# Folding the block-diagonal weights of a recurrent mixer into its gate and score weights, taking square roots on the raw sums, and a later start for a scaling on GpSimd

## The reference, cut to what matters

```python
def block_diag_linear(x, w):                      # w: 512 blocks of 4 x 4
    xb = x.reshape(x.shape[:-1] + (nb, bi))
    return jnp.einsum('...ni,nio->...no', xb, w).reshape(x.shape[:-1] + (nb * bo,))

def mlstm_block(h, w_up, conv_w, conv_b, wq, wk, wv, w_gates, b_gates, ...):
    xm, z = jnp.split(h @ w_up, 2, axis=-1)       # 256 x 2048 each
    xc = jax.nn.silu(causal_conv(xm, conv_w, conv_b))
    q = block_diag_linear(xc, wq)
    k = block_diag_linear(xc, wk)
    v = block_diag_linear(xm, wv)
    gates = q @ w_gates[:2048] + k @ w_gates[2048:4096] + v @ w_gates[4096:] + b_gates
    i_pre, f_pre = gates[:, :4], gates[:, 4:]     # log_sigmoid(f_pre): a softplus
    hh = mlstm_chunkwise(heads(q), heads(k), heads(v), i_pre, f_pre)   # 4 heads of 512
    hh = head_layer_norm(hh, norm_g) + skip * xc
    return (hh * jax.nn.silu(z)) @ w_down

def layer_norm(x, g, b):   # (x - mean) * rsqrt(var + 1e-5) * g + b
def rms_norm_2(x, g):      # x * rsqrt(mean(x * x) + 1e-6) * g
```

## Time and profile before

| | us |
|---|---|
| median of 3 runs | 2662.36 |
| the profiled execution, its own time | 2666.65 |
| its span (first to last instruction) | 2664.8 |
| PE busy | 2370.0 (89% of the span) |
| DVE busy | 1746.7 (66%) |
| ACT busy | 1198.4 (45%) |
| POOL busy | 221.5 (8%) |
| granted PE clock, mean | 0.937 of full speed |

### The profile page before, as it was taken

One profiled execution on the slowest core, in us unless ns is written; L12 is line 12 of the kernel. 1 busy time (PEld: TensorE's weight loads), 2 busy tenths in 40 slices (PEclk: granted clock), 3 DMA queues, 4 the chain that ended last, 5 costly groups with the idle time before them and its releaser, 6 DMA issues.

```text
span 2664.8 us, 34633 instructions
## 1 busy us (share of the span) xinstructions
PE 2370.0 (89%) x14138; PEld 2071.4 (78%) x14138; DVE 1746.7 (66%) x2134; ACT 1198.4 (45%) x1410; POOL 221.5 (8%) x234
## 2 busy tenths in 40 slices
PE   5779889996878899997899887899989989998997
PEld 5667778885656778886899786789979989367997
DVE  2557557887477566887776766677667765156554
ACT  2353335674344335675433564243343345343432
POOL 4001001211001001220000012000000020300000
PEclk9788999997798899999999998999999999988999
DMA  7315667894303766897686432368668734003651
GB/s 182 127 69 186 216 221 285 316 329 177 112 1 136 256 236 242 313 329 259 221 278 228 144 111 95 126 227 280 221 215 288 253 124 165 32 1 127 199 189 64
DMA packets 241166, 504.89 MB, mean 189 GB/s; under 512 B 10287, under 2 KB 104497, under 8 KB 241008
## 3 DMA queue, kind: packets, MB, share of 16 engines
q1 hardware_dynamic: 216128, 417.84, 45.3%
q10 hardware_dynamic: 21456, 77.09, 8.2%
q0 software_dynamic: 3424, 7.75, 1.3%
HBM read 501.59 MB, written 1.05 MB: 189 GB/s over the span
## 4 chain that ended last, share of the span: by engine, by line
PE 42%; DVE 7%; ACT 3%; issue 1%; ACTq 0%; DVEq 0%
PE PS L990 19%; PE PS L1005 9%; PE PS L831 5%; PE PS L791 3%; DVE WGL L2131 1%; PE PS L1415 1%; DVE AR L2134 1%; PE PS L1510 1%; PE PS L1027 1%; DVE X L2131 1%; DVE XN L2131 1%; ACT WGH L1598 1%; PE PS L1460 1%; DVE XTL L2131 1%; PE PS L1438 0%
## 5 line engine op out<-in xcount | busy, mean ns | idle before, releaser
L2131 DVE TENSOR_TENSOR WGL<-ring,WGH 128x2048 fp32r<-128x2048 f32 x258 | 589.4, 2289 | 308.0 <-ACT WGH L1598 173.1
L990 PE MATMUL PS<-XTH,WGH 128*128 128x256 f32 x1408 | 403.3, 286 | 7.7 <-DVE XTL L2131 7.6
L990 PE MATMUL PS<-XTL,WGH 128*128 128x256 f32 x1408 | 401.0, 285 | 0.0
L990 PE MATMUL PS<-XTH,WGL 128*128 128x256 f32 x1408 | 400.9, 285 | 0.0
L990 PEld LDWEIGHTS PS<-XTH,WGH 128*128 128x128 f32 x1408 | 272.9, 194 | 13.8 <-issue 9.7
L990 PEld LDWEIGHTS PS<-XTL,WGH 128*128 128x128 f32 x1408 | 272.8, 194 | 4.1 <-issue 1.0
L990 PEld LDWEIGHTS PS<-XTH,WGL 128*128 128x128 f32 x1408 | 272.7, 194 | 0.0
L2131 DVE TENSOR_TENSOR WDL<-ring,WDH 128x1024 fp32r<-128x1024 f32 (+1 forms) x136 | 217.1, 1597 | 63.2 <-ACT WDH L1751 46.3
L1751 ACT ACTIVATE WGH<-ring 128x2048 fp32r<-128x2048 f32 x96 | 183.4, 1912 | 165.6 <-PE PS L1055 99.0
L1598 ACT ACTIVATE WGH<-ring 128x2048 fp32r<-128x2048 f32 (+1 forms) x74 | 138.4, 1876 | 200.6 <-PE PS L813 73.9
L1790 ACT ACTIVATE XN<-PS 128x256 f32<-128x256 f32 x88 | 33.7, 383 | 358.0 <-PE PS L990 326.2
(11 more groups left out here) (494 smaller groups left out, 5357.3 us busy)
## 6 DMA issues: line engine op xcount, KB each, us to landing
FA<-in_ada_w ACTq DMA_DIRECT2D x144, 512.0 KB, 6.3
ring<-in_moe_w_up SPq DMA_DIRECT2D x64, 1024.0 KB, 7.0
ring<-in_moe_w_gate SPq DMA_DIRECT2D x64, 1024.0 KB, 7.3
ring<-in_moe_w_down SPq DMA_DIRECT2D x64, 1024.0 KB, 6.3
ring<-in_ffn_w_gate SPq DMA_DIRECT2D x44, 1024.0 KB, 5.6
ring<-in_ffn_w_up SPq DMA_DIRECT2D x44, 1024.0 KB, 9.4
ring<-in_ffn_w_down SPq DMA_DIRECT2D x44, 1024.0 KB, 7.3
ring<-in_hyb_w_in SPq DMA_DIRECT2D x10, 1152.0 KB, 6.6
```

What stands on the lines that cost most here:

```text
L990: ins = mm(PS[:, 4 + b, m * T:(m + 1) * T], w_[:, b, w], x_[:, k, :], start=k == 0 and q == 0, stop=k == KD - 1 and q == 2)
L2131: return V.tensor_tensor(out_, x_, y_, op)
```

## The change

**Folding.** At the start of the kernel, behind POOL's small loads, ten POOL instructions (L688 to L701 of the changed kernel) multiply the gate weights, loaded now in another layout in 12 loads of 128-byte pieces (`G4`), by the 4x4 blocks, and leave in `WGT` weights that apply to `XC` and `XM` directly; four more loads (`K4`) and the same instructions put the product of the q and k blocks into `WQKV[0]`. The 12 loads of `WGT` are gone. A new semaphore, `fold`, counts to 10; DVE waits for it ahead of the attention of `even` (the loads lie in `XN`), PE ahead of the first gate product. The gates are now 32 products instead of 48 + 48, and they stand within the projection: one behind each of tiles 4 to 19 (with `XM`), four behind each of tiles 13, 16, 20 and 23 (with `XC`). `scores(h)` makes 4 products with ACT copies instead of 8 and uses `XC` as the keys. POOL makes 32 block-diagonal matrices instead of 96. ACT's Silu of `XC` stands at tiles 11, 14, 18 and 21 instead of 21, 24, 27 and 30; the gates are copied out at tile 24 and the softplus Exp stands at tile 25. DVE interleaves its softplus with the low parts of the last five pieces.

**Roots.** `root_of_variance` and `root_of_squares` give epsilon as the Sqrt's bias and (for the squares) 1/D as the Square's scale, so DVE's step on `VAR` and its mark are gone; `root_of_squares` begins with a 1x1 Sqrt ahead of the Squares.

**The scaling by GpSimd** waits, besides the transposes, for `m_route` (DVE's reordering of the routing) ahead of `moe0` and `moe1`, and for `x_low` (all of X split) ahead of `odd`. In `moe`, ACT's `trn_out` stands ahead of two of its high parts.

The diff, cut to its core:

```diff
@@ gpsimd: start of the kernel
-            for g in range(6):
-                for m in range(2):
-                    ld(WGT[:, g, m, :, :], a["mlstm_w_gates_2"][0][8 * g * P:8 * (g + 1) * P, 4 * m:4 * m + 4]
-                       .rearrange("(k p) e -> p k e", p=P), "small_load")
+            for i in range(4):
+                for w in range(3):
+                    ld(G4[i::4, 16 * w:16 * w + 16, :, :].rearrange("n k c e -> n k (c e)"),
+                       a["mlstm_w_gates_2"][0][2048 * w:2048 * (w + 1), :].rearrange("(t n c) e -> n t (c e)", n=32, c=4),
+                       "small_load")
+                ld(K4[i::4, :, :, :].rearrange("n k i c -> n k (i c)"),
+                   a["mlstm_wk_2"][0].rearrange("(t n) i o -> n t (i o)", n=32), "small_load")
...
+            pool.wait_ge(S("small_load"), 16 * N_SMALL)
+            gmul(G4, G4, bc(by_row.unsqueeze(3), (P, 48, 4, 8)), ALU.mult).then_inc(S("fold"), 1)
+            gmul(K4, K4, bc(WQKV[:, 0, :, :].unsqueeze(2), (P, 16, 4, 4)), ALU.mult).then_inc(S("fold"), 1)
...
@@ gpsimd: scaling of the residual
                     pool.wait_ge(S("xt_ps"), 4 * (plan[n + 1].u + 1))
+                    if plan[n + 1].kind == "moe":
+                        pool.wait_ge(S("m_route"), 5 * plan[n + 1].me + 4)
+                    else:
+                        pool.wait_ge(S("x_low"), plan[n + 1].sb + KD // 2)
@@ tensor: mlstm
                 for f in range(32):
                     project_tile(r, f, 6)
...
+                    if f == 4:
+                        pe.wait_ge(S("row"), r.v2 + 1)
+                        pe.wait_ge(S("fold"), N_FOLD)
+                    if 4 <= f < 20:
+                        pe.wait_ge(S("tile_out"), EV_BASE["mlstm"] + f - 3)
+                        gates_add(16 + f - 4, XM[:, f - 4, 3:])
+                    if f in (13, 16, 20, 23):
+                        h = (13, 16, 20, 23).index(f)
+                        pe.wait_ge(S("xc"), h + 1)
+                        for k in range(4 * h, 4 * h + 4):
+                            gates_add(k, XC[:, k, :])
...
-                for h in range(4):
-                    pe.wait_ge(S("bd"), h + 1)
-                    pe.wait_ge(S("xc"), h + 1)
-                    for w in range(3):
-                        for j in range(4):
...
@@ scalar
-            def root(out_, in_):
-                count["sqrt"] += 1
-                act.wait_ge(S("var"), count["sqrt"])
-                f(out_, in_, ACT.Sqrt).then_inc(S("sd"), 1)
+            def root_of_variance(eps):
+                count["var"] += 1
+                act.wait_ge(S("var"), count["var"])
+                f(SD, MV[:, :, 1], ACT.Sqrt, bias=eps).then_inc(S("sd"), 1)
+            def root_of_squares():
+                f(ST[0:1, 94:95], EPSC[0:1, 1:2], ACT.Sqrt)
+                for t in range(TT):
...
+                    f(XN[:, t, :], X[:, t, :], ACT.Square, scale=D ** -0.5, accum_out=SSQ[:, t:t + 1])\
+                        .then_inc(S("ssq"), 1)
+                act.wait_ge(S("ssq"), count["xres"])
+                f(SD, SSQ, ACT.Sqrt, bias=EPSC[:, 1:2]).then_inc(S("sd"), 1)
@@ scalar: mlstm
+                    if f_ == 24:
+                        act.wait_ge(S("gadd"), 32)
+                        f(SPX[4], PS[32:36, 6, 0:T], ACT.Copy).then_inc(S("f_row"), 1)
+                    if f_ == 25:
+                        softplus_exp(SPX[1], SPX[0])
@@ vector: mlstm
-                for p in range(10, r.n_proj + 2):
+                for p in range(10, 13):
                     low(r, p)
...
+                softplus(SPX[5], x_, *SPX[0:4], beside)
+                low(r, 15)
...
                 mark().then_inc(S("gtok_in"), 1)
+                low(r, 16)
+                low(r, 17)
```

More of the change, by code:

```diff
@@ L470, in program @@
         BLK = [(0, P), (P, MW)]
+        roots = []
+        for r in plan:
+            if r.kind in ("ffn", "hyb", "mlstm"):
+                roots.append((r.name, "begin"))
+            if r.name == "odd":
+                roots.append((r.name, "q"))
+            if r.name == "hyb":
+                roots += [(r.name, 0), (r.name, 1)]
+            if r.name == "mlstm":
+                roots += [(r.name, h) for h in range(4)]
+            if r.kind in ("even", "odd", "moe"):
+                roots.append((r.name, "ln"))
+        roots.append(("final", "begin"))
+        ROOT_AT = {x: n + 1 for n, x in enumerate(roots)}
         work = [r for r in plan if r.kind != "mod"]
@@ L1576, in squares @@
             def squares(r):
-                for t in range(TT):
-                    act.wait_ge(S("xres"), TT * r.v2 + t + 1)
-                    f(XN[:, t, :], X[:, t, :], ACT.Square, accum_out=SSQ[:, t:t + 1]).then_inc(S("ssq"), 1)
-                root(SD, VAR)
+                root_of_squares()
                 act.wait_ge(S("rstd"), r.v2 + 1)
@@ L1708, in odd @@
                       PS[0:HD, b, 0:m * T].rearrange("p (m t) -> p m t", m=m), ACT.Copy).then_inc(S("qit"), 1)
-                root(SD4, VAR4)
+                f(SD4, SSQ4, ACT.Sqrt, bias=EPSC[:, 1:2]).then_inc(S("sd"), 1)
                 act.wait_ge(S("odd_ps"), 2)
@@ L2005, in hyb @@
                     if f_ == LRU_AT + 12:
-                        root(RG, RG)
+                        act.wait_ge(S("lru_one"), 1)
+                        f(RG, RG, ACT.Sqrt).then_inc(S("lru_root"), 1)
                     if k == 1:
@@ L2027, in hyb @@
                         high(r, r.n_proj + 4)
-                root(H2_RS[:, 0, :], H2_RS[:, 0, :])
+                act.wait_ge(S("sq_out"), 1)
+                f(H2_RS[:, 0, :], H2_RS[:, 0, :], ACT.Sqrt).then_inc(S("sd"), 1)
                 high(r, r.n_proj + 5)
-                root(H2_RS[:, 1, :], H2_RS[:, 1, :])
+                act.wait_ge(S("sq_out"), 2)
+                f(H2_RS[:, 1, :], H2_RS[:, 1, :], ACT.Sqrt).then_inc(S("sd"), 1)
                 for p in range(r.n_proj + 4, len(r.pieces)):
@@ L2101, in final @@
             def final():
-                for t in range(TT):
-                    act.wait_ge(S("xres"), TT * v2_end + t + 1)
-                    f(XN[:, t, :], X[:, t, :], ACT.Square, accum_out=SSQ[:, t:t + 1]).then_inc(S("ssq"), 1)
-                root(SD, VAR)
+                root_of_squares()
             act.dma_start(CON[:, :], a["const"][:, 0:NCONST]).then_inc(S("con_load"), 16)
@@ L2134, in stt, with inverse, softplus @@
                 return V.scalar_tensor_tensor(out=out_, in0=x_, scalar=s, in1=y_, op0=o1, op1=o2)
-            def root(rstd, sd):
-                count["var"] += 1
-                mark().then_inc(S("var"), 1)
-                dve.wait_ge(S("sd"), count["var"])
+            def inverse(rstd, sd, name, what):
+                dve.wait_ge(S("sd"), ROOT_AT[name, what])
                 c(V.reciprocal(rstd, sd))
-            def softplus(out_, x_, a_, e, d, w):
+            def softplus(out_, x_, a_, e, d, w, beside=None):
                 count["sp"] += 1
@@ L2790, in hyb @@
                         c(stt(RG, H2, 1.0, RG, ALU.add, ALU.mult))
[L2791 to L2792 removed]
+                        mark().then_inc(S("lru_one"), 1)
                         mark().then_inc(S("hyb_made"), 1)
@@ L2937, in mlstm @@
                         c(V.bn_stats(BN[:, t, 0, :], HN[:, t, :]))
-                        c(V.bn_aggr(MV[:, t, :], BN[:, t, 0, :]))
-                    c(ts(VAR, MV[:, :, 1], EPS, None, ALU.add))
-                    root(RSTD, SD)
+                        ins = V.bn_aggr(MV[:, t, :], BN[:, t, 0, :])
+                        if t == 0:
+                            c(ins)
+                    ins.then_inc(S("var"), 1)
+                    inverse(RSTD, SD, "mlstm", h)
                     for t in range(TT):
```

187 lines of the change are left out of this document (87 added, 100 removed).

## The result

The changed kernel takes 2600.26 us (median of 4 runs, 2597.93 to 2606.41) where the kernel before takes 2663.16 (4 runs, 2659.74 to 2664.22): a ratio of 0.9771, 95% interval 0.9756 to 0.9786, so 62.9 us or 2.3% faster. The forecast was 2596 with a range of 2580 to 2613. The profiled execution took 2606.41, the longest of the four; its span is 2604.6 us.

The account below looks back on a forecast made before the run. TensorE's feed-forward and projection products bound the kernel and stay; gains lie between them. Terms 46.3 + 1.5 + 9.5 + 2.8 + 5.3 + 1.7 - 1 = 66.1 us, off the median 2662.36, give 2596; range 2580 to 2613.

Parts of the forecast that it names:

- the likeliest case: Whole kernel: all terms hold and the median falls from 2662.36 to 2596 us; chance 0.46.
- Step 1: mlstm, projection to first pm: softplus hidden, gate products between tiles, stalls of 1.6 and 4.3 us; 46.3 us saved.
- Step 2: Heads of mlstm: PE work halves but the table load waits for the variance; 1.5 us saved, bounds -1 and 5.
- Rival B: Heads: table load not held by the variance, heads 1 to 3 give 1.5 us each; 2593 us, chance 0.15.
- Step 3: Start of odd: late GpSimd scaling no longer stretches DVE's splitting of X; 9.5 us saved, bounds 3 and 10.
- Rival A: Start of odd: GpSimd's port hold moves to low parts, gain 1.5 us instead of 9.5; 2604 us, chance 0.12.
- Step 4: Start of moe0 and moe1: earlier ACT copies and unstretched DVE casts save 1.4 us each, 2.8 in all.
- Step 5: Roots on sums, seven stages: dummy Sqrt hides the table load in four, 1.15 us each, 0.25 elsewhere; 5.3 us saved.
- Step 6: Roots on variances: 0.28 us saved in each of four, plus 0.6 for the hybrid mixer's two roots.
- Step 7: Start of the kernel: some 4 us of GpSimd folding falls on low parts of even's projection; 1 us lost.
- Rivals C and E: C: start loads delay even's first weights, 2601 to 2611, chance 0.1; E: late fold delays even's attention, 2670, chance 0.02.
- Rivals D and F: D: mlstm's projection stalls more, 2601 to 2606, chance 0.1; F: softplus Exp or Silu waits stop PE, 2620, chance 0.05.

Follow-up runs that it names:

- the standard: The changed kernel measured again, unedited, as reference for later runs: 2598.87 us, ratio 0.9764 to the kernel before; its profiled execution took 2592.25 us.
- the first execution: Profiled execution from the first measurement of the changed kernel, with no further edit: 2606.41 us.

## Why the prediction was right

The forecast of the likeliest case came out, 66 us foreseen and 62.9 measured, and the mechanisms were those foreseen, with errors of size in both directions. Step by step:

- **Step 1, mlstm to the first pm**: 46.3 foreseen; 44.2 measured in the standard (185.2 to 141.0 us) and 41.5 in the first execution (143.6). The mechanism held to the single stall: 1.6 and 4.3 foreseen, 1.54 and 4.05 in the trace, and half clock around the second. The forecast counts "the next 12 us" at half clock behind PE's wait in the trace of before; there the clock fell 3.6 us before that wait ended and came back 10 us behind its end. Mis-sized was the term "32 gate products at some 0.5 us", 16 us: they took 19.2. The price of 0.5 holds for the groups (0.51); the 14 lone ones cost 0.73 each, for each brings its own change from fp32r products and back. The rest, from tile 24 to the first pm, was forecast at 41.4 with the clock, and took 40.2 in the standard and 43 in the first execution, where two more stretches of 3.4 us at half clock fell into scores(0). That the clock falls there in one execution and not in the other was in no term.
- **Step 2, the heads**: 1.2 of the 1.5 foreseen lay between the first and the last pm; 1.6 measured. Rival B (the load isn't held) is refuted by the load's row behind the aggregate, and the run that frees it shows what it would have been: 2.75 us more, where the rival had some 3 (2593 for 2596). That the load was held could be read only from the order of instructions, not from the trace of before. The sign of being wrong, a period under 14, was put carelessly: the step itself had 13.1 for head 1, and that came.
- **Step 3, odd**: 9.5 foreseen, 7.7 measured from trace to trace, 6.75 by undoing it. From the transposes to the high part the forecast had 12.5 us, the trace has 14.67. Of the 2.1 between them, 1.3 are the first product, 6.24 us behind the transposes and not 4.93: in odd it waits for ACT's last copy (the 2.57 in its row), in mlstm it didn't. The rest goes with the clock, granted at 0.50 from 641 to 653; at the start of mlstm it was back at full speed 8 us behind the transposes. Why it rose sooner there, no run tells. Rival A (the loss is only moved) is refuted as to time: GpSimd's hold did move to the low parts, but these had idle time ahead of them, and undoing the wait cost 6.75 us up to the high part and 8.0 in the stage.
- **Step 4, the experts' stages**: 1.4 each foreseen; the first expert product comes 2.3 to 2.5 us earlier (14.6 to 12.3 and 12.1), the next high part 1.2 us in moe0 and 2.85 in moe1. So the size was put too low, 2.8 for some 4 in both. The cause was half wrong: the step counted on DVE's casts, "freed of GpSimd's instructions"; with ACT's new order these didn't matter. That late scaling costs nothing there held, though low parts became 4.5 us long.
- **Step 5, roots on sums**: 1.15 a stage foreseen for four, 1.13 measured ahead of mlstm and 1.12 in the three others. All of it is the dummy's; without it the new root is 0.16 slower than the old one. In the three stages without a load 0.23 for 0.25.
- **Step 6, roots on variances**: aggregate to reciprocal 0.59 us before, 0.37 after in odd, and the same in the others: 0.22 each for 0.28.
- **Step 7, the start**: -1 foreseen, nothing to be seen: low parts at 50.91 and 56.67 of 2.29 us, attention's copy at 109.31 for 109.80. The folding's cost on GpSimd was put too low, 4 us for some 8 of its own and 4 of waiting. That GpSimd and not DVE waited is luck of a tenth of a microsecond: where GpSimd was first the low part took 3.87 us, as the sign of the forecast had it. Rivals C and E did not come near.
- **Rivals D and F**: PE waits for no Silu, and the stalls had the size foreseen.

The parts read within stages of the first execution are 41.5 + 1.6 + 7.7 + 3.2 (steps 1 to 4; the high parts of moe0 and moe1 come 1.2 and 2.0 earlier in it), 4.5 and 0.7 for the roots on sums, 0.9 for those on variances. They make 60.1, and the two spans differ by 60.2. That it fits so well is partly luck. In the standard the same parts make some 64 us, and its span is 74.4 us shorter than before: the rest lies where none of these terms stands, among it 2.9 us in the first part of even and 1.7 in each of the short stretches ahead of moe0 and moe1. The two roots of the hybrid mixer, put at 0.6, were not read.

## What to carry to other kernels

Lay out the new order on each engine's queue with durations of the old trace before trusting a sum: both stalls, and the table load that took back most of what the heads won, were visible there. Mending one stall and the load, together with the grouping of the gate products, was worth 14 us on top of the change's 62. When work is hidden beside other work, look at what is queued behind the hiding: low part 14, for which PE waited, stood behind half a series of tiny steps whose result PE wanted only some 13 us after it was there. Preload a table with a dummy where the engine is idle, and put the dummy ahead of the wait, since a load that is placed behind a wait inherits it.
